# State chunks by key half, one row tile for all samples, values by token, and page loads on GpSimd in a decoder layer

## The reference

```
x = x + 0.5 * ffn1(rmsnorm(x));  h = rmsnorm(x);  z = h @ w_in
A: 8 heads x 128, top-3 blocks of 256 keys + own block; a sample has 1024 past keys in 8 pages of 128,
   found through page_table in cache_k / cache_v; T5 bias
B: retention, 4 heads, dk = dv = 256; a sample has a state S[h] of 256 x 256:
   S[h] = gamma[h] * S[h] + k[h] (x) v[h];   o[h] = q[h] @ S[h]
C: attention into 256 memory tokens, 4 heads x 256; prompt: k, v = rmsnorm(mem) @ w_mem_kv;
   a sample has its own cache_mem_k / cache_mem_v
merged = sum over A, B, C of sigmoid(h @ w_gate + b) * (branch @ w_br)
x = x + merged @ w_out;  x = x + 0.5 * ffn2(rmsnorm(x));  y = rmsnorm(x)
```

## Time and the profile before

| | before |
|---|---|
| median of three runs | 2739.36 us (2736.99, 2739.36, 2740.11) |
| profiled execution, its own time | 2738.88 us |
| its span in the trace | 2736.5 us |
| mean granted clock of TensorE | 0.994 |
| busy, share of span: PE, PEld | 98%, 96% |
| busy: VectorE, ScalarE, GpSimd | 56%, 40%, 1% |
| DMA | 601.19 MB, mean 220 GB/s |

### The profile page before, as it was taken

How to read it: one execution, slowest core, us unless ns; L and a number is a source line. 1 busy time by engine, 2 the same in 40 slices (tenths; PEclk the granted TensorE clock), 3 DMA queues, 4 the chain that set the end, 5 groups by cost and what they waited for, 6 DMA issues and landing times.

```text
span 2736.5 us, 51767 instructions
## 1 busy us (share of the span) xinstructions
PE 2683.8 (98%) x22179; PEld 2624.4 (96%) x22179; DVE 1540.7 (56%) x2467; ACT 1094.4 (40%) x967; POOL 36.6 (1%) x66
## 2 busy tenths in 40 slices
PE   7999999999999999999997999999999999999998
PEld 7999999999999999998997988899999999999997
DVE  4545554455447778776773744355555555555455
ACT  6433333333335433554452444344433333333345
POOL 0000000000000000000000000000000000000000
PEclk9999999999999999999999999999999999999999
DMA  7575555555555788799987799756555555555553
GB/s 241 179 254 179 184 185 183 178 178 184 185 168 162 237 294 299 251 355 365 324 305 265 268 310 315 279 170 213 173 182 184 183 179 178 183 185 184 177 158 113
DMA packets 502045, 601.19 MB, mean 220 GB/s; under 512 B 12608, under 2 KB 471584, under 8 KB 500576
## 3 DMA queue, kind: packets, MB, share of 16 engines
q1 hardware_dynamic: 485104, 559.08, 62.6%
q0 software_dynamic: 6528, 25.91, 2.6%
q10 hardware_dynamic: 10240, 13.70, 1.4%
HBM read 575.16 MB, written 25.58 MB: 220 GB/s over the span
## 4 chain that ended last, share of the span: by engine, by line
PE 92%; DVE 3%; DMA 3%; ACT 1%; issue 0%; SPq 0%; POOL 0%; DVEq 0%; ACTq 0%; POOLq 0%
PE PS L497 30%; PE PS L498 29%; PE PS L499 29%; DVE splitL L457 2%; DMA ring<-cache_k 1%; PE PS L1845 1%; DMA ring<-cache_mem_k 1%; DMA raw<-w_gate 1%; PE PS L1364 1%; ACT splitH L451 0%; PE PS L1619 0%; PE PS L1587 0%; DMA grow<-b_gate 0%; PE PS L1228 0%; PE PS L1114 0%
## 5 line engine op out<-in xcount | busy, mean ns | idle before, releaser
L457 DVE TENSOR_TENSOR splitL<-raw,splitH 128x2048 fp32r<-128x2048 f32 (+1 forms) x464 | 1011.9, 2181 | 831.0 <-ACT splitH L451 829.8
L451 ACT ACTIVATE splitH<-raw 128x2048 fp32r<-128x2048 f32 (+1 forms) x464 | 847.7, 1829 | 1519.6 <-PE PS L499 1507.4
L497 PE MATMUL PS<-gH,splitH 128*128 128x264 f32 x3072 | 883.0, 287 | 1.8 <-DVE splitL L457 1.8
L498 PE MATMUL PS<-gL,splitH 128*128 128x264 f32 x3072 | 872.8, 284 | 0.0
L499 PE MATMUL PS<-gH,splitL 128*128 128x264 f32 x3072 | 872.5, 284 | 0.0
L497 PEld LDWEIGHTS PS<-gH,splitH 128*128 128x128 f32 x3072 | 580.9, 189 | 21.0 <-issue 20.6
L498 PEld LDWEIGHTS PS<-gL,splitH 128*128 128x128 f32 x3072 | 581.1, 189 | 0.5 <-issue 0.2
L499 PEld LDWEIGHTS PS<-gH,splitL 128*128 128x128 f32 x3072 | 577.9, 188 | 0.0
L497 PE MATMUL PS<-hH,splitH 128*128 128x264 f32 x1536 | 437.7, 285 | 0.0
L498 PE MATMUL PS<-hL,splitH 128*128 128x264 f32 x1536 | 436.4, 284 | 0.0
L499 PE MATMUL PS<-hH,splitL 128*128 128x264 f32 x1536 | 436.2, 284 | 0.0
(11 more groups left out here) (361 smaller groups left out, 3028.0 us busy)
## 6 DMA issues: line engine op xcount, KB each, us to landing
raw<-ffn_w SPq DMA_DIRECT2D x240, 1024.0 KB, 5.1
raw<-w_in SPq DMA_DIRECT2D x64, 1024.0 KB, 7.6
raw<-w_gate SPq DMA_DIRECT2D x48, 1024.0 KB, 5.9
ring<-cache_k SPq DMA_DIRECT2D x64, 512.0 KB, 7.8
ring<-cache_v SPq DMA_DIRECT2D x64, 512.0 KB, 6.1
raw<-ffn_w SPq DMA_DIRECT2D x32, 768.0 KB, 4.7
raw<-w_mem_kv SPq DMA_DIRECT2D x16, 1024.0 KB, 5.9
raw<-w_out SPq DMA_DIRECT2D x16, 1024.0 KB, 5.5
```

What stands on the lines that cost most here:

```text
L451: nc.scalar.activation(splitH[:, s, tiles, :], raw[:, u, 0:nk, :], ACT.Copy).then_inc(hi_ready, 1)
L457: nc.vector.tensor_tensor(splitL[:, s, tiles, :], raw[:, u, 0:nk, :], splitH[:, s, tiles, :].bitcast(F32), ALU.subtract).then_inc(split_re ...
L497: nc.tensor.matmul(out, w_hi, H[:, k, 0:n], start=first, stop=False)
L498: nc.tensor.matmul(out, w_hi, L[:, k, 0:n], start=False, stop=False)
```

## The change

- Body 1 (`pe_values`) takes the activations as the stationary operand and the weights as 512 moving columns, so that values come out token by feature. The four value turns and their copies on ScalarE go; `values_evac` scales straight into the output tile. `sp_values` loads four rows of tiles of 512 columns per unit in place of eight of 256.
- A chunk holds one half of the keys of all four heads (`state_part`).
- The queries of the states, and the probabilities of the memory, are spread into tiles that are zero but for one column of eight (`q_one`, `M_one`), so that a matmul with eight columns writes eight rows, of which all but the sample's get zero added. All samples accumulate in one group of PSUM rows; there is one row copy, one turn and one copying out for the states and one for the memory (`MEM_ROWS, PAST_ROWS = 1, 2`). The rows of cache values stay as they were (`dve_past_row_out`).
- Loads of pages and queries move from SP's list to GpSimd's (`pool_pages`). GpSimd's list gets the steps T; the entries that it had are set into steps (`pool_step`), after the pages of the step.

```diff
+    def state_part(states, i):
+        return states[i // 2:i // 2 + 1, :, i % 2 * P:(i % 2 + 1) * P, :].rearrange("a h p e -> p (a h) e")
...
+    def dve_one_query(dve, link):
+        dve.wait_ge(st_sent[0], 32)
+        dve.wait_ge(st_sent[1], 32)
+        link(nc.vector.memset(q_one[:, :], 0.0))
+        nc.vector.tensor_copy(q_one[:, :].rearrange("p (t c) -> p t c", t=BT)[:, :, 0:DEC * DEC:DEC + 1],
+                              qrT[:, :, SEQ:N]).then_inc(row_zero, 1)
...
     def pe_chunk(pe, i):
         b = i // 2
         pe.wait_ge(s_new, i + 1)
         if i == 0:
-            pe.wait_ge(row_zero, 1)
-        if i % 2 == 0 and b:
-            pe.wait_ge(row_sb, b)
-        for dt in range(2):
-            for hh in range(2):
-                h = 2 * (i % 2) + hh
-                last = nc.tensor.matmul(PS[32 * h:32 * h + 1, 4, 0:R_DV], qrT[:, 2 * h + dt, SEQ + b:SEQ + b + 1],
-                                        chunk[i % CHUNKS][:, hh, dt, :], start=dt == 0, stop=dt == 1)
+            pe.wait_ge(row_zero, 2)
+        for h in range(R_HEADS):
+            c0 = DEC * (DEC * (2 * h + i % 2) + b)
+            last = nc.tensor.matmul(PS[32 * h:32 * h + DEC, 4, 0:R_DV], q_one[:, c0:c0 + DEC],
+                                    chunk[i % CHUNKS][:, h, :], start=i == 0, stop=i == 2 * DEC - 1)
         last.then_inc(s_read, 1)
...
     def pe_mem_values(pe, b):
         if b == 0:
             pe.wait_ge(d_prob, 1)
-        pe.wait_ge(row_sb, MEM_ROWS + b)
+            pe.wait_ge(row_sb, MEM_ROWS)
         for g in range(2):
             s = page_there(pe, ("MV", b, g))
             for h in range(M_HEADS):
-                last = nc.tensor.matmul(PS[32 * h:32 * h + 1, 4, 0:M_DH], DM["L"][:, b, g, h:h + 1],
-                                        ring[:, s, h * M_DH:(h + 1) * M_DH], start=g == 0, stop=g == 1)
+                c0 = DEC * (M_HEADS * (2 * b + g) + h)
+                last = nc.tensor.matmul(PS[32 * h:32 * h + DEC, 4, 0:M_DH], DM["one"][:, c0:c0 + DEC],
+                                        ring[:, s, h * M_DH:(h + 1) * M_DH], start=b == 0 and g == 0,
+                                        stop=b == DEC - 1 and g == 1)
             last.then_inc(page_used[s], 1)
...
-        for b in range(DEC):
-            if T == MEM_AT[b] + 1:
-                dve_row_out(dve, MEM_ROWS + b, DM["oS"], 0)
+        if T == MEM_AT[DEC - 1] + 1:
+            dve_rows_out(dve, MEM_ROWS, DM["oS"])
...
+    def pe_values(pe, B, between):
+        for c in range(2):
+            pe.wait_ge(pair_free[c], 2 * B)
+            for u in range(4):
+                s, _ = split_slot(c, u, UK, False)
+                pe.wait_ge(split_ready, 8 * B + 4 * c + u + 1)
+                for tt in range(2):
+                    out = PS[:, 2 * c + tt, :]
+                    for j in range(4):
+                        k = 4 * u + j
+                        w_hi, w_lo = by_512(splitH[:, s, :, :])[:, j, :], by_512(splitL[:, s, :, :])[:, j, :]
+                        t_hi, t_lo = memH[:, k, tt * P:(tt + 1) * P], memL[:, k, tt * P:(tt + 1) * P]
+                        nc.tensor.matmul(out, t_hi, w_hi, start=u == 0 and j == 0, stop=False)
+                        nc.tensor.matmul(out, t_hi, w_lo, start=False, stop=False)
+                        last = nc.tensor.matmul(out, t_lo, w_hi, start=False, stop=u == 3 and j == 3)
+                last.then_inc(unit_used, 1)
+                between(4 * c + u)
...
+    def pool_pages(pool, T):
         for n in range(len(PAGES)):
             kind, b, g = PAGES[n]
             if (kind, b) in QUERY_AT and g == 0 and T == QUERY_AT[kind, b]:
-                sp_query(sp, kind, b)
+                sp_query(pool, kind, b)
             if T == LOAD_AT[n]:
-                sp_page(sp, n)
+                sp_page(pool, n)
...
+        for T in range(T_END):
+            pool_pages(pool, T)
+            pool_step(pool, T)
```

More of the change, by code:

```diff
@@ L210, in build @@
     orL = at("orL", [BT, N], H1, F32R)
-    chunk = [at(f"chunk{k}", [2, 2, R_DV], D0 if k == CHUNKS - 1 else A_X + 4096 * k) for k in range(CHUNKS)]
+    chunk = [at(f"chunk{k}", [R_HEADS, R_DV], D0 if k == CHUNKS - 1 else A_X + 4096 * k) for k in range(CHUNKS)]
     vB = at("vB", [2, BR_W], A_EV)
[L215 to L218, removed]
+    orowS = at("orowS", [1, 2, P], D0 + 4096)
+    orS = at("orS", [BT, DEC], D0 + 5120)
+    orS2 = at("orS2", [BT, DEC], D0 + 5376)
+    nS = at("nS", [3, R_HEADS * DEC], D0 + 5632)
+    q_one = at("q_one", [BT * DEC * DEC], D0 + 6016)
     kaT = at("kaT", [BT, N], H2)
@@ L254, in dec_tiles @@
         g += 8 * DEC * heads * 4
+        if kind == "M":
+            t["one"] = at("M_one", [DEC * (pages * heads * DEC + 1)], g + 512)
         t["oS"] = at(f"{kind}_oS", [BT, DEC], g)
@@ L1329, in act_chunk @@
         act.wait_ge(s_in[k], 16 * (i // CHUNKS + 1))
-        for h in range(2):
-            last = nc.scalar.activation(chunk[k][:, h, :, :], chunk[k][:, h, :, :], ACT.Copy, scale=GAMMA[2 * (i % 2) + h])
+        for h in range(R_HEADS):
+            last = nc.scalar.activation(chunk[k][:, h, :], chunk[k][:, h, :], ACT.Copy, scale=GAMMA[h])
         last.then_inc(s_scaled, 1)
@@ L1399, in pe_row_turn, with dve_rows_out, dve_past_row_out @@
         last.then_inc(row_turned, 1)
-    def dve_row_out(dve, n, out, pitch):
+    def dve_rows_out(dve, n, out):
         dve.wait_ge(row_turned, n + 1)
         for et in range(2):
-            c0 = et * (P + pitch)
-            last = nc.vector.tensor_copy(out[:, et:BT:2, n % DEC:n % DEC + 1],
-                                         PS[:, turn_bank(n), c0:c0 + 3 * (32 + 2 * pitch) + 1:32 + 2 * pitch].unsqueeze(2))
+            rows = PS[:, turn_bank(n), et * P:(et + 1) * P].rearrange("p (h c) -> p h c", h=4)
+            last = nc.vector.tensor_copy(out[:, et:BT:2, :], rows[:, :, 0:DEC])
+        last.then_inc(row_out, 1)
+    def dve_past_row_out(dve, k, out):
+        dve.wait_ge(row_turned, PAST_ROWS + k + 1)
+        for et in range(2):
+            c0 = et * (P + 1)
+            last = nc.vector.tensor_copy(out[:, et:BT:2, k:k + 1],
+                                         PS[:, turn_bank(PAST_ROWS), c0:c0 + 3 * 34 + 1:34].unsqueeze(2))
         last.then_inc(row_out, 1)
@@ L1761, in dve_logits @@
             page_read(dve, ("M", DEC - 1, 1))
+            link(nc.vector.memset(t["one"][:, :], 0.0))
             link(nc.vector.tensor_scalar(L[:, :, :, :], S[:, :, :, :], K.scale, None, ALU.mult))
@@ L1823, in dve_probs @@
             last = nc.vector.tensor_tensor(t["L"][:, :, g, :], t["L"][:, :, g, :], t["x1"][:, :, :], ALU.mult)
+        if K is DKM:
+            link(last)
+            w = K.pages * K.heads
+            last = nc.vector.tensor_copy(t["one"][:, :].rearrange("p (b c) -> p b c", b=DEC)[:, :, 0:DEC * w:DEC],
+                                         t["L"][:, :, :, :].rearrange("p b g h -> p b (g h)"))
         last.then_inc(d_prob, 1)
```

244 lines of the change are left out of this document (137 added, 107 removed).

## The result

| | before | changed |
|---|---|---|
| median, range | 2739.74 us (2736.99 to 2741.36) | 2713.05 us (2709.50 to 2713.57) |
| profiled execution, its span | 2738.88, 2736.5 us | 2709.50, 2707.8 us |
| mean granted clock | 0.994 | 0.996 |

The ratio is 0.9901, with an interval of 0.9884 to 0.9918: about 1% faster, 26.7 us by the medians. 2707 us was forecast; the time is inside the stated range, at the edge of the forecast's own 2700 to 2713. The profiled execution is the fastest of the four: the others took 2712.7 to 2713.6 us, at granted clocks of 0.994 and 0.995.

What follows compares the result with a forecast made beforehand. TensorE, busy 98% of the span, was taken as the bound; 1.4 + 4.6 + 6.6 + 2.8 + 14.7 + 2.3 = 32.4 us off gave 2707 us. Forecast 2700 to 2713 (0.60), stated range 2698 to 2719.

Steps and rivals of the forecast that it cites:

- The loop through SyncE's queue: Steps 83 to 99: key page, VectorE, split, weight issue, next page in turn; moving pages to GpSimd helps recover 14.7 us.
- memory turns: Memory rows turned once for all samples, not one by one; part of 2.8 us for 14 row turns saved.
- the late weights: Stalls at 1544 and 1549 us behind a weight load queued after pages on SyncE: gain 2.3 us, bounds 0 to 4.1.
- the row tile: TensorE's waits until VectorE copied the previous sample's row out (L1406): 8.7 us to go, if pages are not too late.
- the clock's 3.0 us: Steps 83 to 99: TensorE at 1.2 instead of 2.4 GHz after two long stalls; 3.0 us, expected to go.
- page A7/1: Key page waiting for step 89's memory values to free its slot, delaying step 92's split: 3 us of waiting stay.
- Chunks and row turns of the states: Chunks take 0.55 us to the next matmul instead of 0.96, 6.6 us over 16; fewer row turns add to that.
- the rival of the transfers: Chunk stage: if 369 GB/s is the DMA ceiling, up to 6 us come back; 2710 to 2714 us, chance 0.10.
- The signs named ahead: Trace signs listed beforehand: right, such as clock 1.00 in steps 83 to 99; wrong, such as split waits between 1180 and 1400 us.
- 512 columns: Body 1: 192 matmuls of 512 columns, 0.216 us apart, replace 384 of 256; gain 4.6 us, bounds 0 to 4.6.
- A value turn: After body 1: four turns of four transposes go, 0.36 us each, 1.4 us in all.
- The slower rival: GpSimd becomes the page ring's bottleneck through register-addressed pages; at 20 us per page 2750 us, chance 0.06.

Runs made afterwards that it cites:

- pages_only: The kernel before with page and query loads moved to GpSimd's queue alone: 2723.5 us, ratio 0.9944.
- rows_only: The kernel before with chunks by key half and one row turn each for states and memory, pages still on SyncE, values as before: 2733.08 us, ratio 0.9976.
- the second profile: The changed kernel, unaltered, run and profiled once more beside other kernels: span 2711.5 us, median of runs 2712.82 us, ratio 0.9902.
- keys_later: The changed kernel with one half page of keys fewer at step 89 and one more at step 98: 2707.07 us, ratio 0.9884.
- va_76_keys: The changed kernel, half a key page moved from step 89 to 98, prompt-value stores moved to step 144 (output) and behind step 76's pages (scratch): 2707.10 us.
- bulk_1k: The changed kernel with three of GpSimd's four 1 MB copies at 1325 to 1331 us cut into quarters of 256 columns: 2714.73 us, ratio 0.9914.

## Why the prediction was right, and where its steps were off

**Faster, for the reason given.** The loop through SyncE's queue was the cause of most of the waits in steps 83 to 99. pages_only and rows_only show it from both sides: 18.7 us from the pages alone, nothing from the rows there. Forecast for that stretch were 14.7 us, 1.4 us for memory turns and 2.3 us for the late weights behind it, 18.4 in all; measured 18.5, and 17.2 in the second profile. But the working named the row tile as the place of 8.7 us and let the pages carry only the rest. The caution in it (this part hangs on the pages too) was the true sentence; of the memory's rows and their 1.4 us of turns no time shows a gain, with pages on either queue.

That 18.5 meets 18.4 so closely is luck in part. The stretch of steps 83 to 99 itself became 16.0 us shorter: TensorE's idle time in it fell by 11.6 us (14.75 to 3.13), the low clock cost 1.5 us instead of 3.0, and 2.9 us came out of the time in which TensorE is busy, where only 1.4 us of turns had been counted. By the prediction's own terms, idle time and clock, that is 13.1 us for 14.7: it let the clock's 3.0 us go entirely although a wait of 3 us was to stay, and that wait made the clock fall again. What else shortened the busy time no run shows; each wait ends with a matmul of 0.28 us where the next start would have come after 0.12, which for five waits less is an estimated 0.8 us.

**The 3 us that stay.** The one wait that was worked out ahead, page A7/1 in front of the split of step 92, came at 3.13 us for the forecast 3. From the freed slot to the landing it took 7.4 us for 7.3: 1.0 us to the start of the issue (0.8 had been allowed; half of it is L1556, which reads the row number into a register) and 6.4 us from there to the landing (6.5). keys_later shows that it was this page and no other: moving one half page took the wait and its clock away.

**Chunks and row turns of the states.** 8.0 us forecast, 7.9 and 8.2 measured, each chunk 0.55 us. rows_only, which has them without the rest, gives 7.7. The chunk stage runs at 373 GB/s and gave nothing back there (TensorE is busy 99.79 of 100 us), so the rival of the transfers, with 369 GB/s as the ceiling, did not come there.

**The step that failed: late weights.** "the reloads stay, so I take 2.3, bounds 0 to 4.1". The waits at 1544 and 1549 us did shrink, from 2.95 to 0.7 us; these 2.2 us are part of the 18.5 above. But at steps 72 and 73, where 1.2 us of waits stood that could only go, 3.8 us were lost (3.6 in the second profile): 1.6 us lost in all, outside the bounds. The page loads, set beside the weights on another queue, take bandwidth packet for packet for as long as there are pages to load; in the old queue they stood behind the weights, and only the copies did so, for some 6 us. The prediction put at nothing what transfers that are wanted later cost those wanted now. The new queue alone is enough for the loss: pages_only, in which TensorE does not arrive earlier, lost 3.9. rows_only, 8 us earlier with the old queue, lost 1.3; why the two don't add up in the changed kernel is open. A sign of being wrong that the prediction had named came with it: TensorE waited for splits between 1180 and 1400 us.

**The signs named ahead.** Of the right ones came: no wait for the row tile, a stretch of 84.31 us for some 85, 0.55 us behind a chunk. Missed were the clock of 1.00 in the stretch (0.98), VectorE's wait of less than 20 us (20.2) and 0.216 us for 512 columns. Of the wrong ones the waits for splits came, and at the same place pages that took well over 10 us to land: 13.8 us (median) for the four pages of memory keys issued between 1330 and 1350 us.

**Mis-sized: 512 columns.** 0.227 us (median), not 0.216, between the bounds: 384 x 0.120 - 192 x 0.227 = 2.5 us instead of 4.6, and 2.3 measured over the whole body. A value turn gave 0.45 us instead of 0.36, 1.8 for 1.4: the prediction measured it up to the first matmul behind the turn, but the one after that also comes late, at 0.20 instead of 0.12 us (behind the turn of the earlier trace rows it starts at 109.98). 4.1 us for a forecast of 6.0.

**The sum.** 4.1 + 7.9 - 3.8 + 18.5 = 26.7 us against a forecast of 32.4, and 26.7 by the medians. The 28.7 us between the two profiled executions contain another 2 us of chance: 0.5 at the start and 1.5 of clock at 174 us in the trace of before. That fall also stands against the prediction's "elsewhere it is 1.00", which its rows show only for 1200 to 1300 us.

**GpSimd as the place for page loads.** The slower rival did not come: pages land in 6.0 (`cache_k`) and 5.5 us (`cache_v`), quicker than from SyncE (7.8 and 6.1), and an issue costs 0.53 us. Source line L1560 of the changed kernel (ns of one instruction, least, median, most):

```profile
L1560 POOL DMA_DIRECT2D ring<-cache_k x64: 527/528/577, 953.2 to 1484.1; - x64
...
L1560 POOL DMA_DIRECT2D ring<-cache_mem_k x16: 528/528/565, 1290.8 to 1364.1; - x16
```

The lock of which the Trainium skill warns (page "SBUF — State Buffer", section "SBUF: two separate sides") shows in none of these issues, with VectorE busy for 57% of the span, nor in the landings. How much of VectorE's work here is in a two-port mode no view tells, so the runs don't speak for a kernel with more of it.

## What to carry to other kernels

When several waits share a stretch, look for the loop that the chain of waits goes round, and ask of each wait which other would take it over: two parts of this change were aimed at the same microseconds, and one of them had them all. A load that leaves an in-order queue for a queue of its own no longer stands behind what that queue issues first: it now competes with the transfers that used to go first, and where the DMA engines are full that costs the more urgent one. A slot that is freed and wanted again in the same step is worth moving by one turn: that was 4 to 6 us for two digits in a table. And a transfer that is moved later takes what waits for it along: look for the waits before you move it, as the store of va_76_keys shows.

## What the runs showed of the hardware

**The clock can fall without a wait, in some executions and not in others.** At about 171 us TensorE has just made ten narrow products for the bias table, 2.7 us in which it is never idle. In 5 of 14 profiled executions it soon after ran at 1.2 instead of 2.4 GHz for some 3.4 us, which costs 1.5 us; in the other nine it did not, with the same instructions there. The windows of the second profile of the changed kernel, after those products and after the wait at step 72:

```profile
170.68:174.13 3.45, 3.45 (x18) 3.45 (x18) 1.39 (x5) 0.00 (x0) 0.55 (x1) 0.53 0.42 124
1354.93:1358.42 3.49, 3.49 (x19) 3.49 (x18) 2.61 (x10) 0.00 (x0) 0.53 (x1) 0.51 1.05 374
```

In the first profile of the same kernel the clock did not fall at either place, though it had waited as long at the second (2.46 and 2.37 us). Much of the difference between executions of one kernel is of this kind: counted as matmuls 0.22 us apart instead of 0.12, the stretches at the lower clock cost about 2.9 us in the first profile and 7.0 us in the second. At about 20 us, behind an idle stretch of 4 to 5 us, the clock was at the lower level in every one of the 14 and cost 1.2 to 2.3 us.

**Rows of 1 KB don't make packets of 1 KB** on GpSimd's queue: cut into 256 columns (bulk_1k) the copies still went in packets of 4096 bytes, so the share of a neighbour was not changed by this shape. SyncE's weight loads, with rows of 1 KB, did go in packets of 1 KB.

**512 moving columns save some 5%** against two matmuls of 256: 0.227 us against 2 x 0.120 (medians of body 1).
